# Other places in the on-chip memory for the buffers of a two-block transformer kernel

## The chip, the core and the metric

The kernel runs on one core of a Trainium2 chip. A core has a matrix engine (TensorE, "PE", with its weight loader "PEld"), a vector engine (VectorE, "DVE"), a scalar engine (ScalarE, "ACT"), GpSimd ("POOL") and a queue engine (SyncE, "SP"), and transfers between the large memory and the on-chip memory go through 16 DMA engines. The on-chip memory has 128 partitions, and a buffer lies at the same byte range in each of them. The metric is the time of one execution on the device, in microseconds.

## What is computed

The reference puts two different transformer blocks behind each other, for 256 tokens of width 2048, all in float32.

```python
# first block
h = _rmsnorm(x, attn_norm_w[l])
proj = jnp.einsum('bsd,de->bse', h, w_in[l])            # 2048 -> 8192
y_rec = _hgrn2_mixer(...)                               # gated recurrence, both directions
y_conv = _short_conv_mixer(b_gate, c_gate, h_conv, conv_w[l])
x = x + jnp.einsum('bse,ed->bsd', mixed, w_out[l])
g, u = jnp.split(jnp.einsum('bsd,df->bsf', _rmsnorm(x, ffn_norm_w[l]), w_gate_up[l]), 2, axis=-1)
x = x + jnp.einsum('bsf,fd->bsd', jax.nn.silu(g) * u, w_down[l])
# second block, on _rmsnorm(x, final_norm_w)
ada = (c_act @ w_ada + b_ada)[:, None, :]               # 6 x 2048 modulation values
h = _rms(x, g_norm1) * (1 + sc1) + sh1
proj = h @ w_in                                         # 2048 -> 8256
y_a = _mla_attention(q, k, v)                           # latent attention, 8 heads
y_b = _stick_breaking(q_sb, k_sb, v_sb)                 # 8 heads
merged = jax.nn.sigmoid(gl_a) * (y_a @ w_proj_mla) + jax.nn.sigmoid(gl_b) * (y_b @ w_proj_sb)
x = x + gt1 * (merged @ w_out)
x = x + gt2 * ((jax.nn.silu(gate) * up) @ w_ffn_out)    # 2048 -> 2 x 5632 -> 2048
```

## The kernel before

Every weight matrix is streamed once, in chunks of 256 rows by 512 columns (512 KB) into a ring of four places, `raw`. ScalarE rounds a chunk into `hi` (L329), VectorE takes the rest into `lo` (L335), and TensorE makes three products for each of a chunk's four tiles, `hi` with the high part of the activations, `lo` with the high part, `hi` with the low part (L346 to L348). Their sum has float32 precision. The stationary operand of these is `op_hi`/`op_lo` in most stages, `f_hi`/`f_lo` in the two down projections, `lat_hi`/`lat_lo` and `ya_hi`/`ya_lo` in parts of the second block. Each of the 895 chunks passes the same way, and the stages follow each other: input projection with the recurrence and the convolution beside it, output projection, gate and up, down, then the second block with the same parts and two attentions.

Beside this stream the 24 column blocks of `w_ada` arrive in three small rings, each used in some of the stages (`ada_ring0`, `ada_ring2`, `ada_ring3`, 192 transfers), and VectorE multiplies them with the condition (L559, L561).

The order is written out by hand for each engine, and waits are on semaphores with fixed counts. No planner and no pool decides anything. The buffers are placed by hand too. A call of `sb(name, shape)` puts a buffer at the lowest free byte above what is held at that time, and an `ExitStack` that ends gives its bytes back, so that buffers of different stages lie over each other. Names with `gap`, `under` or `align` hold bytes that nobody reads: they only push what follows to its place. At the end `big` holds the region of `proj` for good, and what follows lies over it, up to byte 229,376, the end of a partition.

Three buffers need a word. `turned` holds two 128x128 diagonal matrices of the tokens' scales; both late norms write it (L454) and TensorE multiplies with it (L516). `shared` holds the positional key columns between an accumulator and its transposition (L1831, L2092). And `gate_cols(j)` names the eight blocks of 512 columns in `proj` that hold the sigmoid gates of the second block: seven from column 0 on, the eighth further right. Each gets one Sigmoid (L1841, shown under its helper's line L1718), one product with an accumulator (L2057), and the sum of two goes into the first four (L2061), which TensorE then transposes (L2182).

Of the kernel before, what the change touches and what calls it, by code (L numbers as in the profile page):

```python
# [24 lines left out]
P = 128  # L25
S = 256
TT = S // P
D = 2048
KT = D // P
NB = 512  # L30
# [5 lines left out]
HEADS = DH // P  # L36
# [6 lines left out]
NOPE, ROPE, VD = 128, 64, 128  # L43
# [78 lines left out]
def build_program(nc, a, out):  # L122
    V, A, T = nc.vector, nc.scalar, nc.tensor
    with ExitStack() as ctx:
        def sb(name, shape, dt=F32, stack=ctx):
            return stack.enter_context(nc.sbuf_tensor(name, shape, dt))
# [37 lines left out]


        parts = sb("parts", [P, 2, TT, 4])
        align = sb("align", [P, 48])
        with ExitStack() as use:
            op2_hi = sb("op2_hi", [P, 4, S], F32R, stack=use)
            op2_gap = sb("op2_gap", [P, 7 * 8 * P], stack=use)  # L170
            op2_lo = sb("op2_lo", [P, 4, S], F32R, stack=use)
        with ExitStack() as use:
            ya_lo = []
            for j in range(2):
                sb(f"ya_gap{j}", [P, (56 + j) * P], stack=use)
                ya_lo.append(sb(f"ya_lo{j}", [P, HEADS // 2, S], F32R, stack=use))
        with ExitStack() as use:
            sb("ring0_gap", [P, 8256 + 6144], stack=use)
            ada_ring0 = sb("ada_ring0", [P, ADA_RING, CK, NB], stack=use)
        with ExitStack() as use:  # L180
            turned = sb("turned", [P, TT, P], stack=use)
            sb("xw_gap", [P, 2 * 1024 - TT * P], stack=use)
            xw2 = sb("xw2", [P, TT, D], stack=use)
        with ExitStack() as use:
            sb("shared_gap", [P, 60 * P], stack=use)
            shared = sb("shared", [P, S], stack=use)
        with ExitStack() as use:
            proj = sb("proj", [P, TT, 8256], stack=use)
        xw = proj[:, :, 6144:6144 + D]
# [42 lines left out]
        with ExitStack() as use:  # L232
            with ExitStack() as inner:
                lat_hi = sb("lat_hi", [P, 8, S], F32R, stack=inner)
                lat_lo = sb("lat_lo", [P, 8, S], F32R, stack=inner)
            with ExitStack() as inner:
                m_q = sb("m_q", [P, TT, GH_HEADS, QH], stack=inner)
                m_k = sb("m_k", [P, TT, GH_HEADS, NOPE], stack=inner)
                m_kp = sb("m_kp", [P, TT, GH_HEADS, ROPE], stack=inner)
                m_v = sb("m_v", [P, TT, GH_HEADS, VD], stack=inner)  # L240
                m_qk = sb("m_qk", [P, GH_HEADS, 2 * S], stack=inner)
                m_rt = sb("m_rt", [ROPE, GH_HEADS, 2 * S], stack=inner)
            with ExitStack() as inner:
                s_in = sb("s_in", [P, TT, 3, GW], stack=inner)
                s_qk = sb("s_qk", [P, GH_HEADS, 2 * S], stack=inner)
                s_l = sb("s_l", [P, GH_HEADS, TRI], stack=inner)
                s_n = sb("s_n", [P, GH_HEADS, TRI], stack=inner)
            sb("under_xn", [P, TT * D], stack=use)
            with ExitStack() as inner:
                m_const = sb("m_const", [P, TRI + ROPE // 2], stack=inner)  # L250
                m_pos = sb("m_pos", [P, TT], mybir.dt.int32, stack=inner)
                m_ang = sb("m_ang", [P, 4, TT, ROPE // 2], stack=inner)
                m_kr = sb("m_kr", [P, TT, ROPE], stack=inner)
            with ExitStack() as inner:
                s_b = sb("s_b", [P, GH_HEADS, TRI], stack=inner)
            sb("under_stage", [P, 2 * CK * S], stack=use)
            with ExitStack() as inner:
                m_s = sb("m_s", [P, GH_HEADS, TRI], stack=inner)
                m_pt = sb("m_pt", [P, GH_HEADS, TRI], stack=inner)
                m_r = sb("m_r", [P, 2, TT, GH_HEADS], stack=inner)  # L260
                m_st = sb("m_st", [P, 3, GH_HEADS, TT], stack=inner)
            y_b = sb("y_b", [P, HEADS, S], stack=use)


        with ExitStack() as use:
# [1334 lines left out]
        FREE0 = SB0 + 3 * DH  # L1600
# [7 lines left out]
            return G_GATE + STICK_PER * g  # L1608

        def gate_cols(j):  # L1610
            c0 = j * NB if j < 7 else FREE0 - ROPE
            return proj[:, :, c0:c0 + NB]

        def in2_src(G):
# [199 lines left out]
        def act_second(act):  # L1814
            h2 = lambda g: act_operand(act, OG["h2"], 8, lambda m: mod[:, m:m + 1], lambda m: ada[:, m:m + 1], only=[g])
            merged = lambda g: act_operand(act, OG["merged"], 8, None, only=[g])
            for G in range(G_END):
# [5 lines left out]
                if n is not None:  # L1823
                    if n < 2:
                        act_read2(act, n, proj[:, :, n * LAT:(n + 1) * LAT], ACT.Copy)
                        act_latent_squares(act, n)
                        if n == 1:
                            act_latent_root(act)
                    elif n == 2:
                        done2(act, 2)  # L1830
                        A.activation(shared[0:ROPE], acc[0:ROPE, bank2(2), 0, 0:S], ACT.Copy).then_inc(acc_free[bank2(2)], 1)  # L1831
                    elif n == 3:
                        act_read2(act, n, proj[:, :, SB0:SB0 + NB], ACT.Copy)
                    elif n < 11:
                        if n == 4:
                            act.wait_ge(lt["split"], LG)
                        act_read2(act, n, proj[:, :, (n - 4) * NB:(n - 3) * NB], ACT.Copy)
                    elif n < 16:
                        act_read2(act, n, proj[:, :, SB0 + (n - 10) * NB:SB0 + (n - 9) * NB], ACT.Copy)
                    elif n < 24:  # L1840
                        act_read2(act, n, gate_cols(n - 16), ACT.Sigmoid)  # L1841
# [140 lines left out]
        def dve_second(dve, cd, out_readout):  # L1982
            merged = lambda g: dve_operand(dve, cd, OG["merged"], 8, 0, only=[g])
            for G in range(G_END):
# [67 lines left out]
                if n is not None and 24 <= n < 32:  # L2052
                    done2(dve, n)
                    j, half = (n - 24) // 2, (n - 24) % 2
                    mine, p = gate_cols(j + 4 * half), bank2(n)
                    dve.wait_ge(acc_free[bank2(23)], freed2(23))
                    V.tensor_tensor(mine, mine, acc[:, p], ALU.mult).then_inc(acc_free[p], 1)  # L2057
                    if half:
                        dve.wait_ge(acc_free[p], freed2(n))
                        dve.wait_ge(acc_free[bank2(n - 1)], freed2(n - 1))  # L2060
                        V.tensor_tensor(gate_cols(j), gate_cols(j), mine, ALU.add).then_inc(gated, 1)  # L2061
# [346 lines left out]
```

## Time and profile before

| | us |
|---|---|
| median of 3 runs | 2706.13 (2704.54 to 2706.43) |
| the profiled execution | 2706.13 |
| its span, first to last instruction | 2704.1 |
| PE busy, share | 2664.6, 99% |
| PEld busy, share | 2213.9, 82% |
| DVE busy, share | 1750.9, 65% |
| ACT busy, share | 1305.8, 48% |
| mean granted clock of TensorE | 0.997 |

The span holds 33,965 instructions. Busy shares say which engine is full, the chain of waits says what the end waited for, and a table by stage says where the full engine has gaps. Matmuls are pipelined and their spans overlap, so the mean of a matmul is longer than the time from one to the next. Where one operation appears in several shapes, the views by shape keep them apart.

### The profile page before, as it was taken

How to read it: one execution, taken by the hardware profiler on the slowest of the kernel's cores; microseconds unless marked ns; L12 is line 12 of the kernel's file. 1: busy time of each engine (PE TensorE's matmuls, PEld its weight loads, DVE VectorE, ACT ScalarE, POOL GpSimd, SP SyncE). 2: the span in 40 equal slices, each digit the busy share in tenths (PEclk: the TensorE clock that was granted, in tenths of full speed). 3: DMA queues.
4: the chain of work that ended last, by engine and by line, in shares of the span. 5: the costliest groups of instructions: out<-in, count | busy, mean ns of one | idle time of the engine just before them, and what ended most of it. 6: DMA issues, size and time to landing. Idle time of an engine off the chain costs nothing.

```text
span 2704.1 us, 33965 instructions
## 1 busy us (share of the span) xinstructions
PE 2664.6 (99%) x12453; PEld 2213.9 (82%) x12453; DVE 1750.9 (65%) x2052; ACT 1305.8 (48%) x1546; POOL 3.2 (0%) x9
## 2 busy tenths in 40 slices
PE   8999999999999999999899999999899999999999
PEld 6888888878888888888787888888788888888887
DVE  5788677477676767788775554575576644445565
ACT  5555554354444444445555566644444444444443
POOL 0000000000000000000000000000000000000000
PEclk9999999999999999999999999999999999999999
DMA  7766554678788888888565455555578766665555
GB/s 253 246 205 188 154 150 152 221 242 283 272 281 274 279 273 288 291 282 268 169 205 170 140 165 170 178 182 179 177 250 282 241 191 187 193 186 173 197 191 171
DMA packets 302070, 581.43 MB, mean 215 GB/s; under 512 B 19934, under 2 KB 20280, under 8 KB 301704
## 3 DMA queue, kind: packets, MB, share of 16 engines
q1 hardware_dynamic: 300912, 576.34, 66.0%
q10 hardware_dynamic: 744, 2.27, 0.2%
q0 software_dynamic: 304, 1.33, 0.2%
q8 instruction: 73, 1.20, 0.2%
q14 instruction: 37, 0.30, 0.0%
HBM read 577.76 MB, written 2.10 MB: 214 GB/s over the span
## 4 chain that ended last, share of the span: by engine, by line
PE 93%; DVE 4%; ACT 2%; issue 1%; DMA 0%; SPq 0%; ACTq 0%; DVEq 0%
PE acc L346 29%; PE acc L348 29%; PE acc L347 29%; DVE lo L335 2%; PE ex L1018 1%; PE aux L1039 1%; PE tp L1407 1%; PE aux L575 1%; ACT hi L329 0%; PE tp L516 0%; DVE op_lo L487 0%; PE aux L2122 0%; ACT stage L479 0%; PE aux L2121 0%; DVE op_hi L486 0%
## 5 line engine op out<-in xcount | busy, mean ns | idle before, releaser
L335 DVE TENSOR_TENSOR lo<-raw,hi 128x1024 fp32r<-128x1024 f32 x895 | 1078.3, 1223 | 506.6 <-ACT hi L329 486.0
L329 ACT ACTIVATE hi<-raw 128x1024 fp32r<-128x1024 f32 x895 | 928.2, 1056 | 669.1 <-PE acc L348 538.4
L346 PE MATMUL acc<-hi,op_hi 128*128 128x512 f32 x2752 | 1088.1, 395 | 13.0 <-DVE lo L335 10.2
L348 PE MATMUL acc<-hi,op_lo 128*128 128x512 f32 x2752 | 1073.8, 390 | 0.0
L347 PE MATMUL acc<-lo,op_hi 128*128 128x512 f32 x2752 | 1072.8, 390 | 0.0
L346 PEld LDWEIGHTS acc<-hi,op_hi 128*128 128x128 f32 x2752 | 517.8, 188 | 125.6 <-issue 18.3
L348 PEld LDWEIGHTS acc<-hi,op_lo 128*128 128x128 f32 x2752 | 517.3, 188 | 109.9
L347 PEld LDWEIGHTS acc<-lo,op_hi 128*128 128x128 f32 x2752 | 518.1, 188 | 102.7 <-issue 0.2
L346 PE MATMUL acc<-hi,f_hi 128*128 128x512 f32 x704 | 275.3, 391 | 0.9 <-DVE lo L335 0.8
L561 DVE SCALAR_TENSOR_TENSOR ada_acc<-ada_ring,cact,ada_acc 128x512 f32<-128x512 f32 x360 | 269.7, 749 | 7.3 <-DVE h_a L898 0.3
L348 PE MATMUL acc<-hi,f_lo 128*128 128x512 f32 x704 | 274.0, 389 | 0.0
L347 PE MATMUL acc<-lo,f_hi 128*128 128x512 f32 x704 | 273.9, 389 | 0.0
L1452 ACT ACTIVATE f_hi<-hid 128x512 fp32r<-128x512 f32 x88 | 55.6, 632 | 247.0 <-PE acc L348 247.0
L346 PEld LDWEIGHTS acc<-hi,f_hi 128*128 128x128 f32 x704 | 132.1, 188 | 29.1 <-issue 1.9
L348 PEld LDWEIGHTS acc<-hi,f_lo 128*128 128x128 f32 x704 | 132.1, 188 | 27.7
L347 PEld LDWEIGHTS acc<-lo,f_hi 128*128 128x128 f32 x704 | 132.2, 188 | 27.3 <-issue 0.2
L1473 DVE TENSOR_TENSOR f_lo<-hid,f_hi 128x512 fp32r<-128x512 f32 x88 | 60.9, 692 | 117.5 <-ACT f_hi L1452 117.0
L486 DVE CAST op_hi<-stage 128x512 fp32r<-128x512 f32 x44 | 18.8, 427 | 61.8 <-ACT stage L479 61.6
L820 ACT ACTIVATE h_e<-ex 128x1024 f32<-128x1024 f32 x32 | 32.0, 1025 | 46.1 <-PE ex L1018 43.0
L1300 ACT ACTIVATE hid<-tp 128x512 f32 (+1 forms) x44 | 23.9, 595 | 52.8 <-PE tp L1407 52.8
L685 ACT ACTIVATE proj<-acc,small 128x512 f32<-128x512 f32 x32 | 20.3, 685 | 54.7 <-PE acc L348 54.7
L580 DVE TENSOR_TENSOR ada<-aux,bada 128x4 f32 (+1 forms) x24 | 3.9, 162 | 52.4 <-PE aux L575 52.3
(315 smaller groups left out, 1420.4 us busy)
## 6 DMA issues: line engine op xcount, KB each, us to landing
raw<-w_in SPq DMA_DIRECT2D x257, 512.0 KB, 3.9
ada_ring<-w_ada SPq DMA_DIRECT2D x192, 512.0 KB, 5.1
raw<-w_gate_up SPq DMA_DIRECT2D x176, 512.0 KB, 4.9
raw<-w_ffn_in SPq DMA_DIRECT2D x176, 512.0 KB, 4.5
raw<-w_down SPq DMA_DIRECT2D x88, 512.0 KB, 5.7
raw<-w_ffn_out SPq DMA_DIRECT2D x88, 512.0 KB, 4.3
raw<-w_out SPq DMA_DIRECT2D x64, 512.0 KB, 4.5
raw<-w_proj_mla SPq DMA_DIRECT2D x16, 512.0 KB, 4.1
```

Source lines behind the costliest of these rows:

```text
L329: A.activation(hi[:, k, :, 0:n], raw[:, k, :, 0:n], ACT.Copy).then_inc(hi_ready, 1)
L335: V.tensor_tensor(lo[:, k, :, 0:n], raw[:, k, :, 0:n], hi[:, k, :, 0:n].bitcast(F32), ALU.subtract).then_inc(lo_ready, 1)
L346: T.matmul(dst, lh, hi[:, k, kk, 0:n], start=first and kk == 0, stop=False)
L347: T.matmul(dst, lh, lo[:, k, kk, 0:n], start=False, stop=False)
L348: mm = T.matmul(dst, ll, hi[:, k, kk, 0:n], start=False, stop=last and kk == CK - 1)
L561: ins = V.scalar_tensor_tensor(out=ada_acc[:], in0=ring[:, j, kk], scalar=cact[:, m:m + 1], in1=ada_acc[:], op0=ALU.mult, op1=ALU.add)
L575: mm = T.matmul(aux[:, 1, f:f + 1], ada_acc[:, f * P:(f + 1) * P], ones[:, 0:1], start=True, stop=True)
L820: A.activation(h_e[:, s % 2].rearrange("p d (t h n) -> p (d t) h n", t=TT, h=GH_HEADS), ex.rearrange("p b (h l n) -> p b h l n", h=GH_HEAD ...
L1018: ins = T.matmul(ex[:, 2 * d + t, h * GW:(h + 1) * GW], gg[:, t, d, h * P:(h + 1) * P], levels[:, lev * P:(lev + 2) * P], start=part == 0, ...
L1039: ins = T.matmul(aux[:, s % 2, x4 * P:(x4 + 1) * P], kd[:, x4 * P:(x4 + 1) * P], qd[:, y4 * P:(y4 + 1) * P], start=True, stop=True)
L1452: A.activation(f_hi[:, j % 2], hid[:, 2 * kc:2 * kc + 2, :], ACT.Copy).then_inc(f["sp"], 1)
L1473: V.tensor_tensor(f_lo[:, j % 2], hid[:, 2 * kc:2 * kc + 2, :], f_hi[:, j % 2].bitcast(F32), ALU.subtract).then_inc(lo_done, 1)
```

## The change

It edits the table of buffers, and one column number. With the sizes added up, this is where the buffers start in a partition, in bytes:

| buffer | before | after |
|---|---|---|
| `align` (its end) | 133,632 | 133,504 |
| `proj`, `hid`, `op2_hi` | 133,632 | 133,504 |
| `xw2` | 141,824 | 141,696 |
| `ya_lo0` | 162,304 | 162,432 |
| `op2_lo` | 166,400 | 166,528 |
| `ada_ring2` | 178,688 | 178,560 |
| `ada_ring0` | 191,232 | 191,104 |
| `ya_lo1` | 195,584 | 195,456 |
| `xn`, `lat_hi`, `cv_u`, `g_hi`, `f_g`, `m_q`, `s_in` | 199,680 | 199,552 |
| `f_hi` | 207,872 | 207,744 |
| `stage` | 216,064 | 215,936 |
| `wrow`, `gt_row`, `ada_ring3`, `y_b` | 220,160 | 220,032 |
| `turned` | 133,632 | 228,224 |
| `shared` | 164,352 | 228,224 |
| `raw`, `hi`, `lo`, `op_hi`, `op_lo`, `xres`, `ada_acc` | 16,896 to 132,096 | the same |

133,632 is 261 x 512; 133,504 is 128 bytes less. All other buffers above `align` go down by 128 bytes as well. `turned` and `shared` no longer lie over the region of `proj`; they share a place of their own (one after the other) above `y_b`. The eighth gate block starts at column 6720 of `proj` and not at 6656. Before, its first 64 columns are also the last 64 of the stick-breaking heads' values, which end at 6720 and have been read by then; after, it starts behind them.

Every engine has the same instructions in the same order in both kernels, with the same waits and counts. In seven instructions something else than the buffers' addresses differs: the register arithmetic of a loop on ScalarE (four, another constant address), and the Sigmoid, the product and the sum on the eighth gate block (three, another column).

```diff
-        align = sb("align", [P, 48])
+        align = sb("align", [P, 16])
         with ExitStack() as use:
             op2_hi = sb("op2_hi", [P, 4, S], F32R, stack=use)
-            op2_gap = sb("op2_gap", [P, 7 * 8 * P], stack=use)
+            op2_gap = sb("op2_gap", [P, 8256 - 4 * S], stack=use)
             op2_lo = sb("op2_lo", [P, 4, S], F32R, stack=use)
         with ExitStack() as use:
             ya_lo = []
             for j in range(2):
-                sb(f"ya_gap{j}", [P, (56 + j) * P], stack=use)
+                sb(f"ya_gap{j}", [P, 7232], stack=use)
                 ya_lo.append(sb(f"ya_lo{j}", [P, HEADS // 2, S], F32R, stack=use))
...
         with ExitStack() as use:
-            turned = sb("turned", [P, TT, P], stack=use)
-            sb("xw_gap", [P, 2 * 1024 - TT * P], stack=use)
+            sb("xw_gap", [P, 2 * 1024], stack=use)
             xw2 = sb("xw2", [P, TT, D], stack=use)
-        with ExitStack() as use:
-            sb("shared_gap", [P, 60 * P], stack=use)
-            shared = sb("shared", [P, S], stack=use)
...
-            y_b = sb("y_b", [P, HEADS, S], stack=use)
+            with ExitStack() as inner:
+                y_b = sb("y_b", [P, HEADS, S], stack=inner)
+            sb("under_row", [P, D], stack=use)
+            with ExitStack() as inner:
+                turned = sb("turned", [P, TT, P], stack=inner)
+            shared = sb("shared", [P, S], stack=use)
...
         def gate_cols(j):
-            c0 = j * NB if j < 7 else FREE0 - ROPE
+            c0 = j * NB if j < 7 else FREE0
             return proj[:, :, c0:c0 + NB]
```

## Rows read from the trace of the kernel before

**Rows 1.** The page: busy time of each engine, and TensorE's granted clock.
```profile
PE 2664.6 (99%) x12453; PEld 2213.9 (82%) x12453; DVE 1750.9 (65%) x2052; ACT 1305.8 (48%) x1546; POOL 3.2 (0%) x9
...
PEclk9999999999999999999999999999999999999999
```

**Rows 2.** The page: shares of the chain that ended last, by engine and line.
```profile
PE 93%; DVE 4%; ACT 2%; issue 1%; DMA 0%; SPq 0%; ACTq 0%; DVEq 0%
PE acc L346 29%; PE acc L348 29%; PE acc L347 29%; DVE lo L335 2%; PE ex L1018 1%; PE aux L1039 1%; PE tp L1407 1%; PE aux L575 1%; ACT hi L329 0%; PE tp L516 0%; DVE op_lo L487 0%; PE aux L2122 0%; ACT stage L479 0%; PE aux L2121 0%; DVE op_hi L486 0%
```

**Rows 3.** Stages: busy us of each engine (instructions), granted clock, DMA share, GB/s.
```profile
0.00:60.00 60.00, 49.03 (x216) 39.63 (x217) 33.45 (x46) 33.64 (x45) 0.20 (x4) 1.00 0.80 264
...
600.00:1255.00 655.00, 655.00 (x2988) 544.60 (x2989) 484.54 (x542) 281.94 (x312) 0.67 (x1) 1.00 0.83 279
1255.00:1310.00 55.00, 46.19 (x209) 38.21 (x208) 40.21 (x55) 32.22 (x52) 0.00 (x0) 0.94 0.56 186
1310.00:1900.00 590.00, 587.91 (x2785) 485.22 (x2784) 348.34 (x394) 327.14 (x433) 2.34 (x4) 1.00 0.56 177
1900.00:1960.00 60.00, 53.09 (x230) 43.96 (x229) 32.73 (x40) 25.05 (x35) 0.00 (x0) 0.91 0.53 172
```

**Rows 4.** Single lines: each operation's count, least/median/most ns, starts, shapes.
```profile
L2061 DVE TENSOR_TENSOR proj<-proj x4: 1224/1224/1225, 1785.9 to 1853.7; 128x1024 f32<-128x1024 f32 x4
...
L2182 PEld LDWEIGHTS tp<-plain,proj x32: 138/139/141, 1789.7 to 1861.5; 128*128 128x128 f32 x32
```

**Rows 5.** The groups that write and use `turned`, by shape.
```profile
L454 DVE TENSOR_SCALAR turned<-plain,small 128x128 f32<-128x128 f32 x4 | 1.0, 283 | 0.1
...
L516 PE MATMUL tp<-turned,xw 128*128 128x128 f32 x32 | 5.9, 352 | 7.4 <-DVE turned L454 7.4
```

**Rows 6.** The costliest groups: busy us, mean ns, idle before and its releasers.
```profile
L346 PE MATMUL acc<-hi,op_hi 128*128 128x512 f32 x2752 | 1088.1, 395 | 13.0 <-DVE lo L335 10.2 <-issue 1.3 <-DVE op_lo L487 1.3
L335 DVE TENSOR_TENSOR lo<-raw,hi 128x1024 fp32r<-128x1024 f32 x895 | 1078.3, 1223 | 506.6 <-ACT hi L329 486.0 <-DVE ada_acc L561 2.6 <-DVE f_a L1358 2.5
...
L329 ACT ACTIVATE hi<-raw 128x1024 fp32r<-128x1024 f32 x895 | 928.2, 1056 | 669.1 <-PE acc L348 538.4 <-DMA raw<-w_gate_up 70.6 <-DMA raw<-w_ffn_in 26.9
```

**Rows 7.** Groups on VectorE and ScalarE, off and on a 512-byte multiple.
```profile
L1145 DVE SCALAR_TENSOR_TENSOR cv_y<-cv_u,cols,cv_y x16: 476/484/486, 427.6 to 471.3; 128x256 f32<-128x256 f32 x16
...
L561 DVE SCALAR_TENSOR_TENSOR ada_acc<-ada_ring,cact,ada_acc x360: 743/751/755, 67.9 to 2135.8; 128x512 f32<-128x512 f32 x180
...
L486 DVE CAST op_hi<-stage 128x512 fp32r<-128x512 f32 x44 | 18.8, 427 | 61.8 <-ACT stage L479 61.6
...
L1148 DVE CAST op_hi<-cv_y 128x256 fp32r<-128x256 f32 x8 | 2.4, 294 | 0.3
...
L479 ACT ACTIVATE stage<-tp 128x256 f32<-128x256 f32 x16 | 5.3, 381 | 16.8 <-PE tp L2182 16.8
...
L1132 ACT ACTIVATE cv_u<-aux 128x256 f32<-128x256 f32 x4 | 1.5, 386 | 4.8 <-PE aux L1122 4.8
```

**Rows 8.** TensorE's groups with operands that move.
```profile
L346 PE MATMUL acc<-hi,f_hi 128*128 128x512 f32 x704 | 275.3, 391 | 0.9 <-DVE lo L335 0.8
...
L346 PEld LDWEIGHTS acc<-hi,f_hi 128*128 128x128 f32 x704 | 132.1, 188 | 29.1 <-issue 1.9
...
L1058 PE MATMUL tp<-proj,h_c 128*128 128x128 f32 x32 | 6.2, 275 | 0.0
...
L1705 PE MATMUL aux<-s_b,s_in 128*128 128x128 f32 x16 | 3.1, 273 | 0.0
```

**Rows 9.** DMA issues of 60 to 420 us, then of 600 to 1255 us.
```profile
ada_ring<-w_ada SPq DMA_DIRECT2D x23, 512.0 KB, 4.8
...
raw<-w_gate_up SPq DMA_DIRECT2D x153, 512.0 KB, 4.9
ada_ring<-w_ada SPq DMA_DIRECT2D x116, 512.0 KB, 5.2
raw<-w_down SPq DMA_DIRECT2D x80, 512.0 KB, 5.7
```

## The prediction

> **What bounds the kernel now.** I read the page's engine shares first: TensorE's matmuls are busy 2664.6 of 2704.1 us, and its granted clock stands at 9 tenths or more of full speed (2.4 GHz) in all 40 slices [rows 1]. The chain of waits says the same in another way: 93% of the way to the end is TensorE, and three lines, the three products of each split-float32 weight chunk (L346 to L348), hold 87% [rows 2]. The table by stage then shows where the other 39.5 us lie: 11.0 in the first 60 us, 8.8 around the norm at 1255 to 1310, 6.9 around the norm at 1900 to 1960, and next to nothing in the long stages (0.0 of 655 us, 2.1 of 590); the remaining 10.7 are in the stretches not shown, the end among them [rows 3]. So a change of this kernel shows in the time only if it lengthens or shortens a matmul, or one of those few short stretches, or if it makes some feed so late that the full stages get gaps.
>
> The profiled execution took 2706.13 us, which is its span of 2704.1 and 2.0 us around it. It is also the median of the three runs shown (2704.54 to 2706.43), so a difference made against the profile needs no correction. A difference of 0.2% is 5.4 us, and that is about the least that a measurement of this kernel can tell from none.
>
> **The change, part by part.** I take the edits by what each could do to an instruction.
>
> 1. No instruction, wait or transfer is added, removed or moved. Each engine has the same sequence, every semaphore the same counts. Thus no wait of the table before goes and none comes; the buffers that move are waited for as before. Moving `turned` and `shared` out of the bottom of the large region frees nothing that somebody waits for, because no wait is written differently. Cost 0 by construction, at both ends.
>
> 2. `gate_cols(7)` is 64 columns further right. It is named by one Sigmoid out of PSUM, one product with PSUM on VectorE, one sum into the fourth merged block, and nothing else: the transposes of L2182 read blocks 0 to 3 only, which this edit leaves alone. Shapes are the same. The four sums take 1224/1224/1225 ns as least, median and most [rows 4], and one of them is the sum with this block. With that length for each of the three they last 3.7 us together, and VectorE is busy 348 of the 590 us of that stage [rows 3], beside a TensorE that is full. Even 10% on them would be 0.4 us, hidden. I take 0.
>
> 3. `turned` (1 KB) and `shared` (1 KB) move to the very top of the partition. `turned` is on the path: TensorE waits 7.4 us for L454 before L516 at the first of the two norms, and 32 products read it there. One write takes 283 ns, one use 352 ns [rows 5]. Both places start at a multiple of 128 bytes; the rows below compare buffers at both ends of the partition without a difference. The bounds of that: 5 ns on each of 4 writes and 64 reads, 0.3 us, or none. I take 0. `shared` is written once and read twice.
>
> 4. All that lies above `align` moves down by 128 bytes, except that `ya_lo0` and `op2_lo` go up by 128. Before, these tiles start at a multiple of 512 bytes, now 128 bytes off one. This is the only part with reach. What it does **not** touch is most of the time: `raw`, `hi`, `lo`, `op_hi`, `op_lo`, the residual and the ADA accumulator stay, so the products with `op_hi`/`op_lo` (2752 in each of three groups, of which one is shown), the 895 splits on VectorE and the 895 on ScalarE keep every address [rows 6]. What it does touch:
>
> - VectorE and ScalarE. The trace has tiles that are already off such a boundary. `cv_u` is read by L1145 at shifts of 0 and 8 bytes, and `cv_y` starts 32 bytes off a 512-byte multiple. L1145 takes 476 to 486 ns for 256 columns in all 16 cases, whichever shift. Its sister L561 on even boundaries takes 751 ns for 512 columns; L335 takes 1223 for 1024 [rows 6], 0.92 ns a column more, by which 256 columns would be 515 and not 484, so the offsets cost nothing. ScalarE writes `cv_u` 4 bytes off, in 386 ns, against 381 into the even `stage`. VectorE's casts are its fastest form, and they keep that from the uneven `cv_y`: 294 ns for 256 columns beside 427 for 512 from `stage` is 0.52 ns a column, where L335 has 0.92 [rows 7]. So the bound from these rows is 0 to 5 ns on an instruction, and nothing below zero is seen. Priced at 5 ns on each of the 88 `f_hi` and 88 `f_lo` writes, this is 0.9 us beside a full TensorE. On the path are only the few steps at each norm: some 30 instructions by 5 ns, 0.15 us. I take 0, nearest to the sixteen equal ones.
>
> - TensorE's weight loads. `f_hi`, `f_lo`, `lat_hi`, `ya_lo` and the transposed blocks move. No row shows TensorE reading 128 bytes off a 256-byte multiple, so I bound it. At the low end nothing. At the high end a load of 512 bytes touches three pieces of 256 and not two, and takes 188 x 1.5 = 282 ns. The cover is thinner than the products' 390 ns suggest, since their spans overlap: the loader of the `f_hi` group is busy 132.1 us and idle 29.1 us before 704 loads [rows 8], 41 ns each, so one load and product come every 229 ns. A load may grow by 41 ns for nothing; at 282 it is 53 over, for 2112 loads of `f_hi` and `f_lo` 112 us. I take 0: loads of `f_hi` are 188 ns on the mean, and L2182 loads both halves of `proj`, of which the second lies 33,024 bytes further and so 256 off a 512-byte multiple, in 138/139/141 ns [rows 4].
>
> - TensorE's streamed operands. Of those that move there are 22 groups of products (attention, the recurrence's outputs, `turned`, `diag`), 6.2 us the largest and 3.1 the smallest, and 89.3 us summed [rows 8]. By the same reasoning the high end is half of that, 45 us. For 5.4 us each would have to be 6% longer. I take 0, as on the two other engines.
>
> - Transfers. The three rings of `w_ada` (192 transfers of 512 KB) are the only large landing place that moves; the weights' own ring stays. `ada_ring0` starts 256 off a 512-byte multiple, `ada_ring2` does not, and their medians to landing are 4.8 and 5.2 us, the first in the stage with the lower DMA load [rows 9]. So nothing speaks for an offset that costs. If each took 6% more, the DMA share of the full stage would go from 0.83 to 0.83 x (1 + 0.06 x 116/349) = 0.85. I take 0.
>
> Sum: 0 + 0 + 0 + 0, with 0.15 us for the norms' steps at the most likely worst: 2706.1 us.
>
> **The rivals.**
>
> (a) *Slower: the ADA rows land badly.* Place: 600 to 1255 us, where the DMA engines are busy 0.83 and 116 of 349 large transfers go to a moved ring. Splits of `raw` chunks there already wait for their transfer (70.6 us on ScalarE, absorbed today) [rows 6, 9]. It decides when the share reaches 1, which needs ADA transfers to cost 1 + 0.17/0.83 x 349/116 = 1.62 times as much. Doubled, the demand is 0.83 x 1.33 = 1.10, and the stage lasts some 68 us longer: 2774. Against it: 128 bytes are a small part of a 2 KB row. The Trainium skill (DMA: Bandwidth & Descriptors, How a descriptor splits into AXI transactions) says a read must start at a 256-byte boundary, so that a row which starts off one fetches bytes that it throws away; by its count a 2 KB row would be 68 beats and not 64, if the landing side were held to the same, which it doesn't say. No row here shows that side. Chance 1%.
>
> (b) *Slower: the loader becomes the bound in the down projections.* Place: the 2112 products with `f_hi`/`f_lo`, 484 us of the kernel at 229 ns each. It decides from 229 ns a load; at 282 it adds 112 us, and the streamed operands 45 at most: 2863, or 2818 by the loads alone. For it speaks that the loader is the second busiest unit (82%) [rows 1] and has 41 ns of room. Against it are the steady loads above and the other two engines, which don't feel 4, 8 or 32 bytes. Chance 3%.
>
> (c) *Faster: two engines no longer meet in the memory.* If today's tiles, all at the same offset in 512 bytes, got in each other's way, offsets of 384 beside 0 would ease it. It would have to show as 0.43 ns on each of the 12,453 matmuls to be 5.4 us: 2700. Against it: an instruction whose company changes all through the run keeps its time (L561: 743/751/755 from 68 to 2136 us, on three rings of which one starts 256 off a 512-byte multiple) [rows 7], and the products with `f_hi` (391 ns), whose tile moves, are no longer than those with `op_hi` (395), whose tile stays [rows 6, 8]. Chance 3%.
>
> **How the numbers follow.** The forecast, no difference, has 93%: it is the sum, and no row contradicts it. Slower by over 0.2% is (a) and (b), 4%; faster (c), 3%. The range need not reach the rivals. It takes the runs shown (2704.5 to 2706.4) and some 4 us on each side, since another launch on another chip may sit elsewhere within 0.2%: 2701 to 2711.
>
> **What the changed profile would show.** Right: the same counts on each engine, L561 near 751 ns, the f_hi loads near 188, L516 near 352, L2061 near 1224, `w_ada` landing within 5 to 5.3 us, and PE at 2664 us within 2. Wrong by (a): ScalarE's waits for `raw<-w_gate_up` well over 70.6 us, and PE under 655 in that stage. Wrong by (b): loads of `f_hi` above 188 ns and near 229, and products over 275 ns in the attention's groups. Wrong by (c): a shorter L346 in the groups whose tiles did not move.

## The result and the profile after

The changed kernel takes 2720.17 us (median of 5 runs, 2719.81 to 2722.43), the one before 2706.38 (2704.54 to 2706.58): a ratio of 1.0055, interval [1.0040, 1.0069]. It is slower by 14 us, 0.5%. I had forecast no difference with 93% and a range that ended at 2711.

The page of the changed kernel, its busy line and its chain of waits, which answer to [rows 1, 2]:

```profile
span 2719.3 us, 33965 instructions
PE 2679.6 (99%) x12453; PEld 2217.3 (82%) x12453; DVE 1750.0 (64%) x2052; ACT 1305.0 (48%) x1546; POOL 3.2 (0%) x9
...
PE 94%; DVE 3%; ACT 2%; issue 1%; DMA 0%; SPq 0%; ACTq 0%; DVEq 0%
```

The counts are the same. The span grew by 15.2 us and TensorE's busy time by 15.0, VectorE's and ScalarE's not at all: what was added is TensorE's own. The groups by shape say which of its products it is. (L347 to L349 here are L346 to L348 of before.)

```profile
L347 PE MATMUL acc<-hi,op_hi 128*128 128x512 f32 x2752 | 1088.9, 396 | 12.7 <-DVE lo L336 9.7 <-issue 1.3 <-DVE op_lo L488 1.1
L348 PE MATMUL acc<-lo,op_hi 128*128 128x512 f32 x2752 | 1073.6, 390 | 0.0
...
L347 PE MATMUL acc<-hi,f_hi 128*128 128x512 f32 x704 | 279.0, 396 | 0.5 <-DVE lo L336 0.5
L348 PE MATMUL acc<-lo,f_hi 128*128 128x512 f32 x704 | 277.8, 395 | 0.0
L349 PE MATMUL acc<-hi,f_lo 128*128 128x512 f32 x704 | 277.8, 395 | 0.0
...
L347 PEld LDWEIGHTS acc<-hi,f_hi 128*128 128x128 f32 x704 | 132.6, 188 | 31.8 <-issue 1.4
```

The products with `op_hi` stay at 390 and 395 to 396 ns, those with `f_hi` and `f_lo` went from 391 and 389 to 396 and 395, while a weight load is still shown with 188 ns and the loader's idle time before the `f_hi` loads grew from 29.1 to 31.8 us [rows 6, 8]. Since the spans overlap, the distance from start to start says more. The timeline of TensorE in the first down projection (start in us, length in us), first of the kernel before, then of the changed one:

```profile
1099.74 0.39 PE L346 MATMUL acc<-hi,f_hi 128*128 128x512 f32 x1
1099.97 0.39 PE L347 MATMUL acc<-lo,f_hi 128*128 128x512 f32 x1
1100.19 0.39 PE L348 MATMUL acc<-hi,f_lo 128*128 128x512 f32 x1
...
1101.10 0.39 PE L346 MATMUL acc<-hi,f_hi 128*128 128x512 f32 x1
```

```profile
1100.10 0.39 PE L347 MATMUL acc<-hi,f_hi 128*128 128x512 f32 x1
1100.33 0.39 PE L348 MATMUL acc<-lo,f_hi 128*128 128x512 f32 x1
1100.56 0.39 PE L349 MATMUL acc<-hi,f_lo 128*128 128x512 f32 x1
...
1101.49 0.39 PE L347 MATMUL acc<-hi,f_hi 128*128 128x512 f32 x1
```

Six products take 1.36 us before and 1.39 after. Over both down projections, the mean of the intervals from one product's start to the next one's (those under 260 ns, which leaves the waits out) was 226.9 ns and is 232.4. The stages' lengths, from the starts of their first and last products, add it up:

| stretch | before, us | changed, us |
|---|---|---|
| first down projection (1056 products with `f_hi`/`f_lo`) | 246.1 | 251.4 |
| second down projection (1056) | 243.8 | 249.5 |
| products with `lat_hi`/`lat_lo` (168) | 38.8 | 39.7 |
| products with `ya_hi`/`ya_lo` (192), and the others between them | 77.9 | 78.6 |
| all before the first down projection (96 with `op2_hi`/`op2_lo`) | 1048.4 | 1048.9 |
| from the norm's products to the latent ones | 84.1 | 85.9 |

The first five rows make 13.1 us, all in products whose stationary tile moved against the streamed ones. Of the fifth row these are the 96 with `op2_hi`/`op2_lo`, which the trace counts in the `op_hi` and `op_lo` groups: 227.0 ns from start to start before, 232.7 after, which is 0.5 us. (The row as a whole moves by 1 us between profiles; e1 below has 1049.6.)

The last row, 1.8 us, is TensorE's clock. Around the first late norm, first of the kernel before, then of the changed one (start and length of a stretch, then the engines' busy time; the third number from the right, 0.78 and 0.56, is the mean granted clock):

```profile
1304.20:1309.40 5.20, 4.56 (x22) 3.78 (x21) 2.24 (x4) 2.04 (x4) 0.00 (x0) 0.78 0.00 0
...
1306.86 0.40 PE L347 MATMUL acc<-lo,op_hi 128*128 128x512 f32 x1
1307.10 0.40 PE L348 MATMUL acc<-hi,op_lo 128*128 128x512 f32 x1
```

```profile
1310.20:1317.10 6.90, 6.26 (x21) 5.02 (x21) 2.24 (x4) 1.96 (x4) 0.00 (x0) 0.56 0.00 0
...
1312.99 0.63 PE L348 MATMUL acc<-lo,op_hi 128*128 128x512 f32 x1
1313.41 0.63 PE L349 MATMUL acc<-hi,op_lo 128*128 128x512 f32 x1
```

TensorE stands idle for 7.4 us at this norm [rows 5], and its first products behind it run at the lower of the two clock levels, 1.2 GHz. In the kernel before the clock is back when the chunk products start, and they follow each other after some 230 ns; in the changed kernel's profile seven intervals are still 427 ns long. The second group of products with `turned` and the third are 5.4 us apart in the one and 7.2 in the other. The same happens without the change: at its second norm the kernel before has 7.0 us there (7.3 after the change, the last 0.3 us of the 15.2), e9 below has 5.4 at both norms, and e1, whose moved tiles lie as in the changed kernel, has 5.4 at the first. Differences of 2 us between runs are of this size, and nothing here ties it to the layout.

What I had expected to stay did stay. The uses of `turned` take as long as before [rows 5], the convolution's products and the product sums too [rows 4, 7]:

```profile
L517 PE MATMUL tp<-turned,xw 128*128 128x128 f32 x32 | 5.9, 352 | 7.3 <-DVE turned L455 7.3
```

```profile
L1146 DVE SCALAR_TENSOR_TENSOR cv_y<-cv_u,cols,cv_y x16: 476/484/486, 427.9 to 471.5; 128x256 f32<-128x256 f32 x16
```

The transfers of `w_ada` land in 5.1 us (5.1 before), and ScalarE's wait for `w_gate_up` is 64.5 us and not 70.6 [rows 6]: rival (a) is out.

### The profile page after: what moved, and what is told of

It reads as the page before. It is cut to its first block, busy times and chain, and to the rows that moved or that the text cites. A ratio compares the mean times of both kernels' runs of the same rounds, so it can differ in the third digit from the quotient of the medians.

```text
span 2719.3 us, 33965 instructions
## 1 busy us (share of the span) xinstructions
PE 2679.6 (99%) x12453; PEld 2217.3 (82%) x12453; DVE 1750.0 (64%) x2052; ACT 1305.0 (48%) x1546; POOL 3.2 (0%) x9
## 4 chain that ended last, share of the span: by engine, by line
PE 94%; DVE 3%; ACT 2%; issue 1%; DMA 0%; SPq 0%; ACTq 0%; DVEq 0%
PE acc L347 29%; PE acc L349 29%; PE acc L348 29%; PE ex L1019 1%; DVE lo L336 1%; PE aux L1040 1%; PE tp L1408 1%; PE aux L576 1%; PE tp L517 0%; DVE op_lo L488 0%; ACT hi L330 0%; PE aux L2123 0%; PE aux L2122 0%; ACT stage L480 0%; ACT xn L434 0%
## 5 line engine op out<-in xcount | busy, mean ns | idle before, releaser
L330 ACT ACTIVATE hi<-raw 128x1024 fp32r<-128x1024 f32 x895 | 927.6, 1056 | 669.6 <-PE acc L349 543.9
L347 PE MATMUL acc<-hi,op_hi 128*128 128x512 f32 x2752 | 1088.9, 396 | 12.7 <-DVE lo L336 9.7
L349 PE MATMUL acc<-hi,op_lo 128*128 128x512 f32 x2752 | 1074.6, 390 | 0.0
L348 PE MATMUL acc<-lo,op_hi 128*128 128x512 f32 x2752 | 1073.6, 390 | 0.0
L347 PEld LDWEIGHTS acc<-hi,op_hi 128*128 128x128 f32 x2752 | 518.4, 188 | 125.1 <-issue 18.0
L349 PEld LDWEIGHTS acc<-hi,op_lo 128*128 128x128 f32 x2752 | 517.8, 188 | 110.2
L348 PEld LDWEIGHTS acc<-lo,op_hi 128*128 128x128 f32 x2752 | 518.6, 188 | 102.9 <-issue 0.2
L347 PE MATMUL acc<-hi,f_hi 128*128 128x512 f32 x704 | 279.0, 396 | 0.5 <-DVE lo L336 0.5
L349 PE MATMUL acc<-hi,f_lo 128*128 128x512 f32 x704 | 277.8, 395 | 0.0
L348 PE MATMUL acc<-lo,f_hi 128*128 128x512 f32 x704 | 277.8, 395 | 0.0
L347 PEld LDWEIGHTS acc<-hi,f_hi 128*128 128x128 f32 x704 | 132.6, 188 | 31.8 <-issue 1.4
L349 PEld LDWEIGHTS acc<-hi,f_lo 128*128 128x128 f32 x704 | 132.6, 188 | 31.1
L348 PEld LDWEIGHTS acc<-lo,f_hi 128*128 128x128 f32 x704 | 132.7, 188 | 30.8 <-issue 0.2
```

Source lines behind the costliest of these rows:

```text
L330: A.activation(hi[:, k, :, 0:n], raw[:, k, :, 0:n], ACT.Copy).then_inc(hi_ready, 1)
L347: T.matmul(dst, lh, hi[:, k, kk, 0:n], start=first and kk == 0, stop=False)
L348: T.matmul(dst, lh, lo[:, k, kk, 0:n], start=False, stop=False)
L349: mm = T.matmul(dst, ll, hi[:, k, kk, 0:n], start=False, stop=last and kk == CK - 1)
```

## The experiments

Theory A: a product is slower when its own stationary tile starts off a multiple of 256 or 512 bytes. Theory B: what counts is the distance between the stationary tile and the streamed one, `hi` or `lo`, within 512 bytes. Theory C: the new places of `turned`, `shared` or the gate block cost the time. All kernels differ from one of the two in the buffers' places alone. "Interval" is the mean from start to start within a group, as above.

**e1_base128: the shift alone.**

```diff
-        align = sb("align", [P, 48])
+        align = sb("align", [P, 16])
```

> The kernel before with `align` at 16 columns and nothing else: the whole upper region 128 bytes lower, `turned`, `shared` and the eighth gate block where they were. Theory A (a product takes some 5.5 ns more when its own stationary tile starts off a 256- or 512-byte multiple) and theory B (it is the distance between the stationary and the streamed tile that counts) both say the changed kernel's time, 2720 us (2718 to 2722), with the down projections' products at 232.5 ns from start to start. Theory C (the new places of `turned`, `shared` or the gate block cost the 14 us) says 2706.

Measured: 2721.88 us against 2706.46, ratio 1.0061 [1.0045, 1.0078]. The two down projections last 251.3 and 249.5 us, as in the changed kernel.

```profile
L347 PE MATMUL acc<-lo,f_hi 128*128 128x512 f32 x704 | 277.7, 395 | 0.0
```

`turned` and `shared` still lie over `proj` here and go down by 128 bytes with it. The 128 bytes are the whole of it. C falls.

**e3_op128: only the tiles of the other stages.**

```diff
+        sb("op_pad", [P, 32])
         op_hi = sb("op_hi", [P, KT, S], F32R)
         op_lo = sb("op_lo", [P, KT, S], F32R)
+        sb("op_pad2", [P, 96])
```

> The kernel before with `op_hi` and `op_lo` alone 128 bytes further (32 columns of nothing ahead of them, 96 behind, so that all later buffers keep their place in 512 bytes). A and B: each of the 8256 products with them goes from 227 to 232.5 ns, 45 us more, 2751 us. C: 2706. If only tiles high up in the partition are touched (a theory D), 2706 too.

Measured: 2746.94 us, 1.0153 [1.0133, 1.0173]. `op_hi`'s intervals are 232.6 ns, `f_hi`'s 226.9.

```profile
L349 PE MATMUL acc<-lo,op_hi 128*128 128x512 f32 x2752 | 1086.4, 395 | 0.0
...
L349 PE MATMUL acc<-lo,f_hi 128*128 128x512 f32 x704 | 273.9, 389 | 0.0
```

The slow and the fast group have changed roles: the cost is not tied to the down projections, nor to the height in the partition. 40.5 us of the 45 arrive in the time; the 8160 products at 5.4 ns are 44 us. TensorE waits for `lo` 8.6 us in this group and not 10.2 [rows 6], so a part fell into gaps.

**e4_stream128: only the streamed tiles.**

```diff
+        sb("hi_pad", [P, 32])
         hi = sb("hi", [P, RING, CK, NB], F32R)
         lo = sb("lo", [P, RING, CK, NB], F32R)
+        sb("hi_pad2", [P, 96])
```

> The kernel before with `hi` and `lo`, the streamed tiles, 128 bytes further (and 96 columns of nothing behind), all stationary tiles on their multiple of 512 bytes. A: no difference, 2706. B: every product with them has a distance of 128 off, some 10,600 products by 5.5 ns, 58 us more, 2765.

Measured: 2761.01 us, 1.0205 [1.0185, 1.0225]. All groups are at 232 to 234 ns, though every stationary tile is on a multiple of 512.

```profile
L349 PE MATMUL acc<-lo,op_hi 128*128 128x512 f32 x2752 | 1087.9, 395 | 0.0
...
L349 PE MATMUL acc<-lo,f_hi 128*128 128x512 f32 x704 | 277.9, 395 | 0.0
```

A falls; B said 2765.

**e5_all128: everything off, nothing apart.**

```diff
+        sb("all_pad", [P, 32])
         raw = sb("raw", [P, RING, CK, NB])
```

> The kernel before with everything from `raw` on 128 bytes further, streamed and stationary tiles alike. A: all stationary tiles are off, some 58 us more, 2765. B: no distance changes, 2706.

Measured: 2704.24 us, 0.9996 [0.9986, 1.0007].

```profile
L348 PE MATMUL acc<-lo,op_hi 128*128 128x512 f32 x2752 | 1072.7, 390 | 0.0
...
L348 PE MATMUL acc<-lo,f_hi 128*128 128x512 f32 x704 | 274.0, 389 | 0.0
```

With each tile 128 bytes off a 512-byte multiple, every product is as fast as before. Together with e4 this separates A from B: an address costs nothing, a distance does.

**e6, e7, e8: which distances.** All have `op_hi`/`op_lo` padded as in e3 (by 64, 8 and 96 columns) and `align` at 64, 96 and 128 columns.

```diff
-        align = sb("align", [P, 48])
+        align = sb("align", [P, 64])
+        sb("op_pad", [P, 64])
         op_hi = sb("op_hi", [P, KT, S], F32R)
```

> The kernel before with two distances at once, each in stages of its own: `op_hi`/`op_lo` 256 bytes off the streamed tiles' place in 512 bytes, and everything above `align` (`f_hi`, `f_lo`, `lat_hi`, `ya_lo`) 64 off. Theory B1 (any distance but a multiple of 512 costs 5.5 ns): products with `op_hi` at 232.5 ns and those with `f_hi` too, 2764 us. B2 (a multiple of 256 is free): `op_hi` 227, `f_hi` 232.5, 2719. B3 (only an odd multiple of 128 costs): both 227, 2706.

Measured: 2723.89 us, 1.0066 [1.0046, 1.0086].

```profile
L349 PE MATMUL acc<-lo,op_hi 128*128 128x512 f32 x2752 | 1073.9, 390 | 0.0
L348 PE MATMUL acc<-hi,f_hi 128*128 128x512 f32 x704 | 279.2, 397 | 0.5 <-DVE lo L337 0.5
```

256 bytes apart is as good as 0: B2, by which a multiple of 256 is free. At 64 the interval is 233.4 ns.

> The same with `op_hi`/`op_lo` 32 bytes off and the upper region 192 off. B1 and B2: both groups at 232.5 ns, 2764 us. B3: 2706. A cost that grows with the distance would put `op_hi` (32) well below `f_hi` (192).

Measured: 2758.18 us, 1.0193 [1.0172, 1.0213]. `op_hi` at 32 bytes 233.2 ns, `f_hi` at 192 only 228.9. So the cost doesn't grow with the distance, and 192 is a case of its own; no theory had it.

> The same with `op_hi`/`op_lo` 384 bytes off and the upper region 320 off. B1: both groups at 232.5 ns, 2764 us; B2 the same. If the sign of the distance matters (the experiment with `op_hi` 128 further gave 232.6), 384, that is 128 the other way, differs from it.

Measured: 2761.82 us, 1.0206 [1.0186, 1.0227]. 384 gives 232.4 ns as 128 does, 320 gives 233.3 as 64 does: the period is 256. At 128 the sign therefore makes no difference, but at 64 it does: 192 is 64 the other way, and has 229 ns.

**e2_after_align40: 32 bytes in the changed kernel.**

```diff
-        align = sb("align", [P, 16])
+        align = sb("align", [P, 40])
```

> The changed kernel with `align` at 40 columns and not 16, which is the most that fits below `turned`: the upper region is 32 bytes below its old place and not 128. B1 and B2: any distance costs, 2720 us, the products of the down projections at 232.5 ns. If the cost grows with the distance up to some size, less: a quarter of 14 us would be 2710.

Measured: 2723.22 us, 1.0060 [1.0043, 1.0077], `f_hi` at 233.3 ns. The stationary tiles of the upper region lie 32 bytes below a multiple of 256 here, a distance of 224. A small distance is no better than a large one.

**e10_op192_f160 and e12_op208: is there a better distance than 0?** `op_hi`/`op_lo` 192 bytes off and the upper region 160; then `op_hi`/`op_lo` at 208, cut out of one buffer:

```diff
-        op_hi = sb("op_hi", [P, KT, S], F32R)
+        op_all = sb("op_all", [P, 2 * KT * S + 128], F32R)
+        op_hi = op_all[:, 52:52 + KT * S].rearrange("p (k n) -> p k n", k=KT)
```

> The kernel before with `op_hi`/`op_lo` 192 bytes off and the upper region 160 off. The `f_hi` products at a distance of 192 took 229 ns on the mean, between 227 and 233, so that `op_hi` should take 229: 8256 x 2 ns = 17 us, and `f_hi` at 160 the 232.5 to 233 of all others, 14 us: 2737. If 192 was low by chance of the ring's phase only, 2764.

Measured: 2737.03 us, 1.0112 [1.0094, 1.0131]: `op_hi` 229.1 ns, `f_hi` 233.3. That the estimate met the time to 0.1 us is in part luck: its terms of 17 and 14 us come to 15 and 16 by these intervals.

```profile
L350 PE MATMUL acc<-hi,op_lo 128*128 128x512 f32 x2752 | 1083.8, 394 | 0.0
L349 PE MATMUL acc<-lo,op_hi 128*128 128x512 f32 x2752 | 1078.6, 392 | 0.0
```

> The kernel before with `op_hi`/`op_lo` 208 bytes off the 256-byte multiple, cut out of one larger buffer. It looks for a distance that is better than 0: 192 gave single intervals of 226 ns beside 229 and 232, and 224 gave 233. I expect 229 to 233 ns, 2723 to 2756 us; below 227 would be a faster kernel than the one before.

Measured: 2747.43 us, 1.0151 [1.0132, 1.0169]; the three kinds of interval are 231.9, 232.6 and 232.8 ns. No distance tried is better than 0 or 256. (The trace calls both tiles `op_all` here; L347 to L349 are L346 to L348 of before.)

```profile
L347 PE MATMUL acc<-hi,op_all 128*128 128x512 f32 x2720 | 1088.9, 400 | 11.7 <-DVE lo L336 8.6 <-issue 1.3 <-DVE op_all L488 1.1
L349 PE MATMUL acc<-hi,op_all 128*128 128x512 f32 x2720 | 1077.0, 396 | 0.0
```

**e11_lo128: one of the two streamed rings.**

```diff
+        sb("lo_pad", [P, 32])
         lo = sb("lo", [P, RING, CK, NB], F32R)
+        sb("lo_pad2", [P, 96])
```

> The kernel before with the streamed ring `lo` alone 128 bytes off, `hi` and all stationary tiles on their multiple. If a load meets only the product that stands beside it in the trace, one interval of three is longer, the one that starts with the product of `lo`: 5.5 ns on a third of 10,600, 19 us, 2726. If a load reaches over two products, as the intervals around `ya_lo` in the changed kernel suggest, two of three are longer: 39 us, 2745.

Measured: 2751.63 us, 1.0166 [1.0148, 1.0185]. The three intervals are 232.7, 231.3 and 231.8 ns (the one that starts with `hi` and `op_hi`, with `lo`, with `hi` and `op_lo`): all three are longer, though only one product of three streams a moved tile. Neither expectation has that. The cost is not local to the product whose tile is off.

```profile
L348 PE MATMUL acc<-hi,op_hi 128*128 128x512 f32 x2752 | 1102.4, 401 | 11.9 <-DVE lo L337 8.7 <-issue 1.6 <-DVE op_lo L489 1.1
L350 PE MATMUL acc<-hi,op_lo 128*128 128x512 f32 x2752 | 1085.3, 394 | 0.0
L349 PE MATMUL acc<-lo,op_hi 128*128 128x512 f32 x2752 | 1084.1, 394 | 0.0
```

**e9_after_even: the changed kernel with its distances back at a multiple of 256.**

```diff
-        ada = sb("ada", [P, ADA * 4])
         raw = sb("raw", [P, RING, CK, NB])
...
+        ada = sb("ada", [P, ADA * 4])
         align = sb("align", [P, 16])
```

> The changed kernel with `ada` (384 bytes) allocated just below `align` and not first of all: `raw`, `hi`, `lo`, `op_hi`, `op_lo` and all up to `align` start 384 bytes lower, everything above keeps the changed kernel's place, so that all streamed and stationary tiles are a multiple of 256 bytes apart again while `turned` and `shared` stay at the top. The distance theory with a period of 256: 2706 us or up to 2 below it, with the down projections' products back at 227 ns. If anything of the 14 us came from the new places of `turned`, `shared` or the gate block, that part stays.

Measured: 2704.50 us (11 runs) against 2706.85, ratio 0.9996 [0.9987, 1.0005].

```profile
L347 PE MATMUL acc<-hi,f_hi 128*128 128x512 f32 x704 | 275.5, 391 | 0.9 <-DVE lo L336 0.8
...
L348 PE MATMUL acc<-lo,f_hi 128*128 128x512 f32 x704 | 274.1, 389 | 0.0
```

`turned` and `shared` sit at the top, the gate block is where the change put it, and the 14 us are gone, since all tiles are a multiple of 256 bytes apart again. No version tried is faster than the kernel before by more than the interval.

The distances together (stationary less streamed, modulo 256; mean of the group's three intervals):

| distance, bytes | 0 | 32 | 64 | 128 | 160 | 192 | 208 | 224 |
|---|---|---|---|---|---|---|---|---|
| interval, ns | 227 | 233.2 | 233.4 | 232.5 | 233.3 | 228.9, 229.1 | 232.5 | 233.3 |

## Why the prediction was wrong

**The step that failed** is point 4 under "TensorE's weight loads", where I took 0 with ends of 0 and 112 us. The measured value is 5.5 ns on the mean of 2112 products, 11 us in the two down projections, and 2 us more in the latent, attention and output products: a tenth of the gap between my ends, but 2.5 times what a measurement can tell. The place was right (rival (b) named the down projections), its mechanism was not. I had bounded how much longer *a load* from an uneven address takes. The load is shown with 187 to 189 ns at every offset, and e5 shows that an uneven address by itself costs nothing.

**Two readings led there.** First, all my evidence was of instructions with one tile off a multiple, on VectorE and ScalarE, and of TensorE's loads from `proj` at an offset of 256, the one distance besides 0 that these runs found free (e6). "No row shows TensorE reading 128 bytes off" stood in the text, and behind it should have stood a real share of the chance, not 3%. Second, I called the loader's 41 ns of idle time room in which a load may grow for nothing. In the changed kernel the product starts later while the loader idles more, 31.8 us against 29.1: the loader's idle time was not the slack. What sets the 227 ns is not read from either record. The recurrence's products of 256 columns start 119.6 ns apart, so 256 columns more cost 107 ns; by that 512 are 215, an estimate, and the 12 ns left are there at distance 0. A slip beside it: point 4 let all 2752 products of each `op_hi`/`op_lo` group keep their addresses, but 32 of each use `op2_hi`/`op2_lo`, which moved, for 0.5 us.

**Rival (c)** had the idea of two readers that meet, as a gain and with engines other than TensorE. What the runs show is TensorE's two operands and a loss: 0 and 256 bytes apart is the good case, and these products had it everywhere. The engines beside it don't matter for the difference: of the down projections' intervals during which neither VectorE nor ScalarE is busy (from 240 ns ahead to 160 ns behind), 213 have a mean of 226.7 ns before and 239 one of 232.3 after. Nor do transfers: the intervals without a DMA packet under way, some 160 in each, have 226.7 and 232.1.

**Right were** points 1 to 3 (e1 and e9: `turned`, `shared` and the gate block cost nothing that shows), the VectorE and ScalarE part of point 4, the streamed operands `turned` and those of the attentions (L517 352 ns), and the transfers. The estimate for the time scaled well once the distance was known to count: by the theory that held, e2 to e10 were forecast from 5.5 ns a product (e10 also from 2) within 6 us, of differences up to 55. e11 lies 7 us above the nearer of its two forecasts, and e12 had only a range.

**What stays open.** That the read of the next weights and the read of the streamed columns hinder each other in the on-chip memory is the nearest account, and it is argued, not shown. The Trainium skill (SBUF — State Buffer, Who interferes with whom) gives TensorE two independent read ports, one for the streamed operand and one for the weight loads (LDWEIGHTS), and says that it never waits on anyone. By that rule e3, e4 and e5 would be alike, and they are 2747, 2761 and 2704 us. Against a simple form of the account stands e11, where intervals are longer in which no tile in use is off, and the changed kernel's `ya` products, where only `ya_lo` is off and two of three intervals (232.5 and 233.4 ns beside 227.6) are longer. Nor is the cost the same for each product. In the kernel before 96% of the down projections' intervals are 226 or 227 ns; in the changed one they run through 232, 228, 230, 233, 241, 232 and 231 ns and begin again, after seven products, though the kinds of product repeat after three. No run explains the seven. Shorter products whose operands moved apart by 128 bytes don't pay: those of the recurrence (last section), and the transpositions of `f_a` with 128 columns, 109.0 ns apart before and 108.9 after. They differ from the others in more than length, and no run varies the length alone, nor the row length of 512 bytes of the stationary tile.

## What to carry to other kernels

Where TensorE is full and each product loads new weights, as in these float32r products of 512 columns, keep the stationary tiles and the streamed tiles a multiple of 256 bytes apart in the partition; a buffer inserted or a pad shortened somewhere below can break it for every stage above, with no instruction changed. When a layout edit moves a region, list which operand pairs of the full engine change their distance, and multiply by their count, rather than look at each operand's own alignment. And judge a pipelined product by the time from start to start, not by its record's length or by the loader's idle time.

## What the runs showed of the hardware that I had not expected

A float32r product of 128 x 128 weights with 512 columns follows the last after 227 ns at distances of 0 and 256 bytes, after 232.5 at 128 and 208 and after some 233.3 at 32, 64, 160 and 224, with 229 at 192. The loader's record doesn't show it. The shorter products of the recurrence (256 columns, L1018) behave in another way: 119.2 to 119.6 ns at 0, 119.7 at 128 and 119.8 at 160, but 117.8 at 64, 117.9 at 192 and 116.9 at 224, so for them some uneven distances are slightly better; with 232 such intervals that is under 1 us here.
